# Running sums of the last attention: three float32 matmuls, or six float32r ones of a high and a low term

## The reference

```python
logits = jnp.einsum("bhtd,bhsd->bhts", q[:, :, s0:end], kb) * (Dh ** -0.5)
mask = s_idx[None, :] < t_idx[:, None]
log_keep = jnp.where(mask, jax.nn.log_sigmoid(-logits), 0.0)
after = jnp.sum(log_keep, axis=-1, keepdims=True) - jnp.cumsum(log_keep, axis=-1)
wts = jnp.where(mask, jnp.exp(jax.nn.log_sigmoid(logits) + after), 0.0)
outs.append(jnp.einsum("bhts,bhsd->bhtd", wts, vb))
```

## Time and profile before

| | us |
|---|---|
| median of 3 runs | 872.67 (872.42 to 876.31) |
| the profiled execution | 869.95 |
| its span on the core | 868.2 |
| PE busy | 802.5 (92%) |
| DVE busy | 639.5 (74%) |
| ACT busy | 494.7 (57%) |
| PE, matmuls at L2336, L2337 and L2338 | 10.0, 6.1 and 6.2 |

### The profile page before, as it was taken

How to read it: one execution, slowest core, us unless ns; L and a number is a source line. 1 busy time by engine, 2 the same in 40 slices (tenths; PEclk the granted TensorE clock), 3 DMA queues, 4 the chain that set the end, 5 groups by cost and what they waited for, 6 DMA issues and landing times.

```text
span 868.2 us, 16874 instructions
## 1 busy us (share of the span) xinstructions
PE 802.5 (92%) x7058; PEld 746.4 (86%) x7058; DVE 639.5 (74%) x1286; ACT 494.7 (57%) x1014; POOL 0.2 (0%) x4
## 2 busy tenths in 40 slices
PE   4988899999999999999997699999999889999988
PEld 3977899998998999999996678888888879978888
DVE  4477978887677899887887867867767768954454
ACT  4567754454456666565456565373756456567762
POOL 0000000000000000000000000000000000000000
PEclk8999999999999999999999989999999999999999
DMA  8522565776445566645783412221334237854211
GB/s 339 222 98 97 190 250 181 260 284 222 148 165 194 193 229 230 209 166 212 269 318 135 177 52 97 97 99 50 104 103 162 80 139 264 281 183 146 97 49 49
DMA packets 22684, 148.50 MB, mean 171 GB/s; under 512 B 2640, under 2 KB 3024, under 8 KB 6480
## 3 DMA queue, kind: packets, MB, share of 16 engines
q1 hardware_dynamic: 22608, 147.43, 48.0%
HBM read 146.37 MB, written 1.05 MB: 170 GB/s over the span
## 4 chain that ended last, share of the span: by engine, by line
PE 75%; DVE 15%; ACT 7%; issue 1%; DMA 1%; SPq 0%; DVEq 0%; ACTq 0%
PE ps L1993 56%; DVE wlo L1488 4%; DVE raw L1509 2%; DVE tmp L1485 1%; PE pp L2179 1%; PE pp L2232 1%; PE pp L2252 1%; PE pp L2211 1%; PE pp L2247 1%; PE pp L2170 1%; DVE vt L1485 1%; PE pp L2147 1%; PE pp L2336 1%; PE pp L2347 1%; DMA x<-xT 1%
## 5 line engine op out<-in xcount | busy, mean ns | idle before, releaser
L1993 PE MATMUL ps<-p0hi,whi 128*128 128x256 f32 x1128 | 332.5, 295 | 18.3 <-DVE p0lo L1488 8.2
L1993 PE MATMUL ps<-p0lo,whi 128*128 128x256 f32 x1128 | 319.0, 283 | 0.0
L1993 PE MATMUL ps<-p0hi,wlo 128*128 128x256 f32 x1128 | 318.8, 283 | 0.0
L1488 DVE TENSOR_TENSOR wlo<-raw,whi 128x512 fp32r<-128x512 f32 (+2 forms) x436 | 273.9, 659 | 19.0 <-ACT whi L1089 18.5
L1993 PEld LDWEIGHTS ps<-p0hi,whi 128*128 128x128 f32 x1128 | 216.2, 192 | 31.3 <-issue 15.3
L1089 ACT ACTIVATE whi<-raw 128x512 fp32r<-128x512 f32 (+2 forms) x436 | 238.8, 600 | 3.4 <-DMA raw<-wst 3.4
L1993 PEld LDWEIGHTS ps<-p0lo,whi 128*128 128x128 f32 x1128 | 216.4, 192 | 1.9 <-issue 1.7
L1993 PEld LDWEIGHTS ps<-p0hi,wlo 128*128 128x128 f32 x1128 | 216.2, 192 | 0.0
L1509 DVE CUSTOM_DVE_ANT_0 raw<-raw,cact,vc 128x1024 f32<-128x1024 f32 x64 | 81.8, 1277 | 0.0
L1993 PE MATMUL ps<-zhi,whi 128*128 128x256 f32 x176 | 49.4, 281 | 1.1 <-DVE wlo L1488 1.1
L1993 PE MATMUL ps<-zlo,whi 128*128 128x256 f32 x176 | 48.7, 277 | 0.0
(11 more groups left out here) (348 smaller groups left out, 1357.5 us busy)
## 6 DMA issues: line engine op xcount, KB each, us to landing
raw<-wst SPq DMA_DIRECT2D x125, 1024.0 KB, 5.0
raw<-wsd SPq DMA_DIRECT2D x16, 704.0 KB, 4.3
x<-xT SPq DMA_DIRECT2D x4, 256.0 KB, 4.9
m_x<-memT SPq DMA_DIRECT2D x1, 1024.0 KB, 8.1
outT<-x SPq DMA_DIRECT2D x4, 256.0 KB, 2.4
cact<-cB SPq DMA_DIRECT2D x1, 512.0 KB, 14.2
cst<-con SPq DMA_DIRECT2D x1, 356.0 KB, 12.3
smo<-conr SPq DMA_DIRECT2D x1, 320.0 KB, 11.8
```

Source lines behind the costliest of these rows:

```text
L1488: return v.tensor_tensor(lo, src, hi.bitcast(F32), ALU.subtract)
L1993: ins = t.matmul(o, a, b, start=first and q == 0, stop=last and q == len(ops) - 1, skip_group_check=True)
```

## The change

DVE splits -log_keep after k_sp as weights are split: a copy to float32r (sphi) and the rest (splo), each waiting for its predecessor, and k_sp is ticked by the last. PE multiplies both with float32r copies of ntri and of the column of -1, six matmuls in place of three. A new job k_c, once before k_qk 0, makes these copies on DVE. To make room in SBUF, the tiles g1, g2, rows, cols and acc2, which the last attention does not use, move into a scope that is closed before its tiles are laid out.

```diff
+            if j == 0:
+                add("k_c")
             add("k_qk", j)
...
+        sphi, splo = ([sb(f"{n}{i}", [P, 384], F32R, pq)[:, :] for i in range(4)] for n in ("sphi", "splo"))
+        ntri, minus = sb("ntri", [P, P], F32R, pq)[:, :], sb("minus", [P, 1], F32R, pq)[:, :]
...
-                    stt(l1, ps[3 + 2 * (j % 2) + hh][:, 0:384], 0.0, l1, ALU.max, ALU.add).then_inc(*tick("k_sp"))
+                    hi = sphi[2 * (j % 2) + hh]
+                    own.mark(stt(l1, ps[3 + 2 * (j % 2) + hh][:, 0:384], 0.0, l1, ALU.max, ALU.add))
+                    e.wait_ge(*own.last)
+                    own.mark(v.tensor_copy(hi, l1))
+                    e.wait_ge(*own.last)
+                    low(splo[2 * (j % 2) + hh], l1, hi).then_inc(*tick("k_sp"))
+                elif kind == "k_c":
+                    e.wait_ge(*on("glo", "b", 4))
+                    v.tensor_copy(ntri, C("ntri"))
+                    v.tensor_copy(minus, C("biases", 11, 12)).then_inc(*tick("k_c"))
...
-                    bank, l1 = ps[3 + 2 * (j % 2) + hh], tr[2 * (j % 2) + hh]
+                    bank = ps[3 + 2 * (j % 2) + hh]
                     e.wait_ge(*on("k_sp", j, hh))
-                    t.matmul(bank[:, 0:T], C("ntri"), l1[:, 0:T], start=False, stop=False, skip_group_check=True)
-                    t.matmul(bank[:, P:T], C("biases", 11, 12).broadcast_to([P, P]), l1[:, T:384], start=False, stop=False, skip_group_check=True)
-                    t.matmul(bank[:, T:384], C("ntri"), l1[:, T:384], start=False, stop=True, skip_group_check=True).then_inc(*tick("k_acc"))
+                    for w in (sphi[2 * (j % 2) + hh], splo[2 * (j % 2) + hh]):
+                        t.matmul(bank[:, 0:T], ntri, w[:, 0:T], start=False, stop=False, skip_group_check=True)
+                        t.matmul(bank[:, P:T], minus.broadcast_to([P, P]), w[:, T:384], start=False, stop=False, skip_group_check=True)
+                        ins = t.matmul(bank[:, T:384], ntri, w[:, T:384], start=False, stop=w is splo[2 * (j % 2) + hh], skip_group_check=True)
+                    ins.then_inc(*tick("k_acc"))
```

More of the change, by code:

```diff
@@ L201 @@
     "k_qk": "stick_pe", "k_acc": "stick_pe", "k_av": "stick_pe", "k_log": "stick_act", "k_exp": "stick_act",
-    "k_hi": "stick_act", "k_sp": "stick_dve", "k_cp": "stick_dve", "k_z": "stick_dve", "k_lo": "stick_dve",
+    "k_hi": "stick_act", "k_c": "stick_dve", "k_sp": "stick_dve", "k_cp": "stick_dve", "k_z": "stick_dve", "k_lo": "stick_dve",
     "resb": "resb", "cr": "cr",
@@ L872, in program @@
         p0lo = sb("p0lo", [P, KC, T], F32R)
-        g1 = sb("g1", [P, KC * 8 + 28])
-        g2 = sb("g2", [P, KC * 16 + 24])
         cact = sb("cact", [P, D])
         mod = sb("mod", [P, 64])
-        R0, R1, R2 = (sb(f"rows{i}", [8, 512]) for i in range(3))
-        cols = sb("cols", [P, 64])
         sm = sb("sm", [P, 72])
@@ L884, in program @@
         acc = sb("acc", [P, T])
+        pr = ExitStack()
+        g1 = sb("g1", [P, KC * 8 + 28], c=pr)
+        g2 = sb("g2", [P, KC * 16 + 24], c=pr)
+        R0, R1, R2 = (sb(f"rows{i}", [8, 512], c=pr) for i in range(3))
+        cols = sb("cols", [P, 64], c=pr)
         ph = ExitStack()
@@ L902, in program @@
         ph.close()
-        acc2 = sb("acc2", [P, 2 * T])
+        acc2 = sb("acc2", [P, 2 * T], c=pr)
         pf = ExitStack()
@@ L916, in program @@
         pg.close()
+        pr.close()
         pq = ExitStack()
+        sphi, splo = ([sb(f"{n}{i}", [P, 384], F32R, pq)[:, :] for i in range(4)] for n in ("sphi", "splo"))
+        ntri, minus = sb("ntri", [P, P], F32R, pq)[:, :], sb("minus", [P, 1], F32R, pq)[:, :]
         q1hi = sb("q1hi", [P, KC, T], F32R, pq)
```

## The result

The kernel with the change took 883.21 us (median of 4 runs, 882.95 to 883.67), the kernel before 874.49 in the same comparison (4 runs, 872.42 to 876.87). The ratio is 1.0111 with a 95% interval of 1.0068 to 1.0155: slower, and by twice what was forecast (+8.7 us instead of +4.3). The profiled execution took 882.95 us (span 881.2) against 869.95 (span 868.2).

What follows compares the result with a forecast made beforehand. The prediction took the chain of ACT's logarithm, k_sp and k_acc ahead of PE's stream as the bound. Chain 3.0 plus one clock fall 1.3 makes 4.3 us: 874.3 profiled, 877.0 with the 2.7 median difference; range 873.2 to 880.6.

Steps and rivals of the forecast that it cites:

- what bounds it, and the chain: Last attention: PE's stream waits on a latency chain through ACT's logarithm and DVE's k_sp, which ends 0.98 us later.
- a sum of 0.74: DVE's k_sp: alternative delay if copy and subtraction start without gaps, 0.74 us instead of 0.98.
- the unit: PE, one k_acc (one j, one hh): six float32r matmuls take 0.68 us, 0.78 after a wait, 0.20 us shorter.
- where the two meet: Pairs of j on PE: later k_sp less shorter units puts the projection 0.63 us later in pairs 0/1, 2/3 and 4/5.
- The staggered pair: Pair 6/7, where two waits lie one behind the other: 1.14 us later.
- dearer terms: Rival: copy at 0.49 and short matmuls at 0.17 add 1.7 us more, 878.7 and over; chance 0.06.
- PE is relieved: Rival: 16 x 0.20 us leave PE's stream, DVE's additions lie in its free time, 869.5 us; chance 0.08.
- the change doesn't do what it says: Rival: float32r matmuls cost as float32 and additions overlap, or gain and loss cancel: 872.7 us; chance 0.06.
- a part of PE that waited for a lo behind a pair: Sign of being wrong: DVE's lo, queued behind the waiting copies, delays PE's parts; the forecast took this at nothing.
- the clock: PE's silences for k_sp in pairs 0/1 and 4/5: about one fall to granted 0.50 in the two, costing 1.3 us.
- The two silences: PE's waits for k_sp in pairs 0/1 and 4/5, forecast to lengthen to 2.3 and 2.6 us.
- The rival with two falls: Rival: both lengthened silences are followed by a fall of the clock, 878.3 us; chance 0.22.

Runs made afterwards that it cites:

- g3: Kernel before with only DVE's split added (k_acc still float32) and idle matmuls in PE's silences: attention 82.57 us, no low clock there.
- g1: The changed kernel with idle matmuls in its silences, except ahead of k_acc(2,1): ratio 1.0037 to the kernel before, attention 81.00 us.
- e2: Kernel before with the new tile places and DVE's split alone, PE multiplying in float32, no fill: 883.06 us, 10 us slower than before.
- e3: Kernel before with the new tile places and float32r products alone, k_sp writing float32r without copy or subtraction, no fill: 877.38 us, ratio 1.0046.
- e1: Kernel before with only the tiles laid out as in the changed one, arithmetic unchanged: ratio 1.0009, attention 78.18 us.
- b1: The kernel before run again without any edit, with its own profile: 873.61 us (870.79 to 876.72, 10 runs).
- g4: Kernel before with split and float32r products for hh = 0 only, and idle matmuls in 23 places of the whole kernel: 867.77 us, ratio 0.9934.
- f1: The changed kernel with idle matmuls in its silences, including ahead of k_acc(2,1): 882.64 us.

## Why the prediction was wrong

**Right: what bounds it, and the chain.** The time is set by k_log, k_sp and k_acc one behind the other in front of PE's stream. The copy was taken at 0.37 us (measured 0.360), the subtraction at 0.55 (0.559), the two gaps at 0.03 (796.22 + 0.56 to 796.81, + 0.36 to 797.21, measured 0.03 and 0.04). Their sum was 0.98 us, and g3 measures 0.99 for each of three pairs. What the prediction drew from the Trainium skill (VectorE: DVE Perf Modes, The DRAIN you can't avoid), a sum of 0.74, is not borne out: each waiting operation starts behind the end of its predecessor, as at 8.62 in the earlier trace rows, while one that does not wait starts 0.08 ahead of it (790.69 there).

**Right: the unit.** From 798.21 to 798.55 three float32r matmuls pass, 0.34 us, so a unit is 0.68 as reckoned from the earlier trace rows; behind a wait it is 0.73 (797.82 to 798.55) and not 0.78. That is 0.113 each on average, though four of the six have 128 columns, and hardly less than the 0.117 to 0.119 of the projections, which all have 256. The fast weight load of the Trainium skill (TensorE: Matmul & The Clock Gate, Weight-path perf modes), on for 128 weights whose type is not FP32, shows nothing here: a unit would have been 0.45.

**Right: where the two meet.** 0.63 a pair was forecast, g1 has 0.66, 0.62 and 0.62. The staggered pair was put at 1.14 and took 0.98. Together 2.88 at the end of the pairs and 2.85 for the attention (81.00 - 78.15), where 3.0 was forecast. The rivals "dearer terms", "PE is relieved" and "the change doesn't do what it says" fall with this. Nor was there a part of PE that waited for a lo behind a pair.

**Wrong: the clock.** The step that failed is "So I expect about one fall in the two". The two silences came at 2.31 and 2.72 us for the forecast 2.3 and 2.6, but behind the first the clock was low for 6.8 us and behind the second for 3.4, and a third stretch of 3.4 lay at the silence behind k_z. Counting 3.4 us as one, that is four and not one: three behind the two silences that the change lengthens, and one behind a silence that it leaves alone. Set against g1, which has the same chain without them, after is later by 1.58 us behind pair 0/1, 2.89 behind 2/3, 3.18 behind 4/5 and 4.44 behind 6/7 and at the end of the attention, and 0.64 more in outb (23.38 - 22.74): 5.1 us, 1.3 for each of the four. So the price of a fall was well sized and the number of falls was not: 5.1 less the forecast 1.3 are 3.8 of the 4.4 us by which the difference to before missed. (The median itself, 883.21 against a forecast 877.0, is off by 6.2; the other 1.8 are the kernel before, which stood at 874.49 in this comparison and at 872.67 in the forecast.) By the Trainium skill (TensorE: Matmul & The Clock Gate, Terms), which puts the loss at the low time times the share of the clock that is missing, it would be 6.8 us for 13.6 us. The traces have 5.1: PE is idle for 0.4 us of the three stretches, and the silence ahead of outb takes up 0.67 (0.37 at 853.86, 1.04 at 842.52 in before); where the rest went was not worked out.

What led to it was reading the silences that the change lengthens and none of the others. Not one silence that the change leaves alone was asked about, since the earlier trace rows has the clock at 1.00 behind 839.81. That was the state of one schedule. e2 and e3 show 6.8 us of low clock behind this very silence and 25.1 us of outb instead of 22.7, with a change that ends before it. The other part is that a fall was counted as 3.4 us long, though the trace of before has two of 6.8 among its nine. And the count of the longer silences was short: that trace has not two above 2.4 us but four (2.69 at 14.71, 2.78 at 90.24, 4.02 at 499.27, 2.63 at 701.60), each with low clock at or behind it and two of them with 6.8 us. The silence forecast at 2.6 was of that kind, so one fall in the two was low even by that trace. The rival with two falls was the nearer one, and it too counted only those behind the two lengthened silences. The ends of the range do not follow from their terms either: two falls and half of the dear terms give 879.1 and not 880.6, the chain at 0.74 without a fall about 874.5 and not 873.2. The measured 883.21 lies outside all of these.

**Open.** About 0.6 of the 4.4 us is left, within the intervals. 0.17 is the slower outb with the new places. From 720 to 760 us the float32r matmuls start 119 ns apart (median) in each of the ten kernels with the new places and 117 or 118 in the four profiles with the old ones, which over these 40 us would be some 0.5 us more, but e1's ratio (0.9982 to 1.0036) can't tell it. Why the places matter was not tried. The profile of after also has 44.4 us of low clock ahead of the attention, more than the 37.5 and 34.1 of the first two of before. What decides whether a given silence is followed by a fall is not settled either: before and b1 differ in it at the same silences. Where the falls lie was read from one profiled execution of each kernel; that they recur in the others is shown by the clocks of all executions in their sum, and by the medians: filling moves after by 6.5 us and e3 by 5.4 (1.0046 to 0.9984).

## What to carry to other kernels

Before a split into a high and a low term, find out whether its operations land on an engine with free time or in a chain that another engine waits for: here DVE was half free, and 0.98 us more of it still cost 0.99 a pair, of which the cheaper products gave back 0.36. Where TensorE has silences of one to three microseconds, a change of well under 1% can be masked or doubled by the clock, so compare versions with those silences filled by idle matmuls, and put the fill only where what it waits for has long come. Filling the kernel before was worth 0.95%, three times what the change cost by its chain (2.85 us, 0.3%), and somewhat less than it cost with its falls (1.11%).

## What the runs showed of the hardware that was not expected

- A silence of 1.34 us between two stretches of full work was followed by 3.4 us at 1.2 GHz (e3, 777.6), one of 1.72 in the same kernel and one of 2.29 in b1 by none. Within one kernel, silences of 1.11 and 1.86 us were each followed by a fall in one execution and by none in the other (before and b1), and the stretch at 545.1 us in before came behind 5.0 us of work without a silence. Low stretches lasted 3.4 or 6.8 us.
- Idle matmuls of 128 columns keep most falls away, though not all (52.9 in g4): 260 of them in 22 places brought the granted clock of the profiled execution from 0.978 to 0.995 and the median from 874.45 to 866.64 us.
- Two executions of one kernel pass the same 192 matmuls at the full clock in 21.73 and 22.57 us, about 114 and 118 ns for each, with no wait in either.
- float32r matmuls with a weight load each pass at 0.113 us on average where two of three have 128 columns (798.21 to 798.55 in after), and at 0.118 where all have 256 (outb in b1); idle ones of 128 columns start 0.111 apart on average in f1.
